# A ring of eight half-expert buffers in a hybrid attention and mixture-of-experts layer

## The chip, the cores and the metric

One core of a Trainium2 chip runs the whole layer in one launch. The metric is device time in microseconds of that core, the median over runs.

## The reference

One layer is applied to 1024 latent tokens and 128 context tokens, width 1024, all in f32. What matters here is its second half:

```python
def hier_moe(h, w_coarse, b_coarse, w_fine, b_fine, w_gate, w_up, w_down):
    ...
    a = (jax.nn.silu(jnp.einsum('td,edf->tef', t, w_gate))
         * jnp.einsum('td,edf->tef', t, w_up) * gates[:, :, None])
    y = jnp.einsum('tef,efd->td', a, w_down)
```

There are 4 groups of 8 experts, 32 in all, with inner width 256. Each token goes to two experts of one group. Ahead of it stand adaLN modulation, windowed attention beside a gated short convolution, and an output projection. Behind it come `x + g2 * moe` and `rmsnorm(x, final_g)`. g2 differs between latent and context tokens.

## The kernel before, in words

**Stages.** Modulation, input projection and attention (to about 382 us), output projection with norm and routing (to 536), the 32 experts (to about 857) and the last stage (to 901). The 1152 tokens are nine tiles of 128; tile 8 holds the context tokens.

**Precision.** A product in f32 is split: `hi` is the value rounded to float32r, `lo` is the rest, and three fast matmuls (hi hi, lo hi, hi lo) take the place of a slow one. So each half of an expert's gate and up weights (128 partitions x 2048 f32, 1 MB) is loaded, ACT writes `gu_hi` (L2165), DVE writes `gu_lo` over the raw half (L2279), and PE runs `products` (L2474 to L2476).

**The ring.** `w_gu` has 3 experts x 2 halves. `gu_hi` has two experts: `gu_hi0` and `gu_hi1`. `w_d` (w_down, 1 MB) has three. The tensors `gu_lo` and `w_gu` share one address, as do `yt` (the nine tiles read back in the last stage) and the raw rings.

**Order by engine.** SP issues nearly all plain DMAs, in program order, and waits there. In the experts' stage its loop is:

```python
for n in range(NE):
    if n + 3 < NE:
        for h in range(2):
            sp.wait_ge(s_gu, 2 * n + h + 1)
            load_gu(n + 3, h)
    if 1 <= n and n + 2 < NE:
        sp.wait_ge(s_down, n)
        load_d(n + 2)
```

`s_gu` counts the halves whose products are done, `s_down` the experts whose `down` is done. PE runs for each expert `gate_up(n, 0)`, `turn_a(n - 1)`, `gate_up(n, 1)`, `turn_x(n + 2)` (eight transposes of gathered rows, L2463), `down(n - 1)` (L2508 to L2518). ACT runs `down_high(n - 1)` (L2195), `turned`, `high(n + 2, 0)`, `silu(n)`, `xhigh(n + 2)`, `high(n + 2, 1)`, `blend(n - 1)` (L2202, which reads the latent row of g2); DVE follows with the low parts, the gated product and `out`. Each engine takes its instructions in order. POOL issues the indirect DMAs: `gather(n + 3)` brings an expert's token rows into `xrows` (a ring of three, L2102), `scatter(n - 2)` writes its results to `y_rows` (L2109). Expert 31 is not scattered: PE adds it from SBUF in the last stage. POOL's descriptors live in a room at the bottom of SBUF, 16384 bytes of a partition.

**Before the experts.** After the last tile's projection PE runs `keep_busy` matmuls (L1860), whose result nobody reads, between waits for DVE's choice of experts: prefix sums (L1904 to L1910), `placed` (L1850, twice: the table of row numbers, then that of gates), and then the first `turn_x`. The first six halves and w_down 0 and 1 are loaded from 505 us on (w_down 2 at 384). SP then waits for the second gather and loads both rows of g2 (1 MB, each row spread over all partitions) and final_g (512 KB).

**Last stage.** When the last scatter has landed, SP loads the nine tiles of `yt` in `ORDER`. POOL or DVE adds the two rows of a token, or PE does; PE adds expert 31, DVE adds the residual (and multiplies by the context g2 for tile 8), ACT and DVE do the final norm with final_g, and SP stores.

Of the kernel before, what the change touches and what calls it, by code (L numbers as in the profile page):

```python
# [41 lines left out]
def build(nc, a):  # L42
# [45 lines left out]
    with root:  # L88
        sb = allocator(root)
        PS = root.enter_context(nc.psum_tensor("PS", [P, 8, 512], F32))  # L90
        ident = sb("ident", [P, P])
# [1132 lines left out]
        s_lo = sem("s_lo")  # L1224
        s_wgu = [[sem(f"s_wgu{i}_{h}") for h in range(2)] for i in range(3)]
# [12 lines left out]
        with ExitStack() as st:  # L1238
# [61 lines left out]
            def mix_sync(sp):  # L1300
                def load_gu(n, h):
                    sp.dma_start(w_gu[:, n % 3, h, :], a["w_gu"][n, h]
                                 ).then_inc(s_wgu[n % 3][h], 16)

                def load_d(n):
                    sp.dma_start(w_d[:, n % 3, :], a["w_down"][n]).then_inc(s_wd[n % 3], 16)

                def load(t):
                    if t >= 2:
                        sp.wait_ge(s_x2, t - 1)  # L1310
                    sp.dma_start(xt[t % 2][:], a["x_all"][:, t, :]).then_inc(s_xt[t % 2], 16)
# [24 lines left out]
                for v, col in ((1, shift_col), (2, gain_col)):  # L1336
                    sp.dma_start(col[:], mod_rows[1, v * D:(v + 1) * D].rearrange(
                        "(k p) -> p k", p=P), allow_slow_non_contiguous=True
                        ).then_inc(s_cols, 16)
                sp.wait_ge(s_pv, NB + 1)  # L1340
                load(0)
                load(1)
                spread_rows(1)
                load_d(2)
                for t in range(LAST):
                    if t + 2 < NT:
                        load(t + 2)
# [444 lines left out]
            def mix_tensor(pe):  # L1792
# [107 lines left out]
                keep_busy(4, 3)  # L1900
# [18 lines left out]
                keep_busy(4, 3)  # L1919
# [49 lines left out]
        ORDER = [4, 5, 0, 1, 8, 6, 2, 3, 7]  # L1969
        DVE_SUM = ORDER[1]  # L1970
        POOL_SUMS = ORDER[2:7]
        with ExitStack() as st:
# [5 lines left out]
            g2row = sb6("g2row", [P, 2, D])  # L1978
            fg = sb6("fg", [P, D])
# [4 lines left out]
            gu_hi = [gu_hi0, sb6("gu_hi1", [P, 2, HALF], F32R)]  # L1984
# [13 lines left out]
            held_hi, held_lo = gu_hi[1][:, 0, 0:D], gu_hi[1][:, 1, 0:D]  # L1998
# [29 lines left out]
            with nc.Block() as block:  # L2028
                @block.sync
                def _(sp):  # L2030
# [3 lines left out]
                    def load_gu(n, h):  # L2034
                        sp.dma_start(w_gu[:, n % 3, h, :], a["w_gu"][n, h]
                                     ).then_inc(s_wgu[n % 3][h], 16)

                    def load_d(n):
                        sp.dma_start(w_d[:, n % 3, :], a["w_down"][n]).then_inc(s_wd[n % 3], 16)

                    sp.wait_ge(s_gx[1], 16)
                    sp.dma_start(g2row[:].rearrange("p c n -> p (c n)"),
                                 mod_g2.to_broadcast([P, 2 * D])).then_inc(s_g2row, 16)
                    sp.dma_start(fg[:], a["final_g"].to_broadcast([P, D])).then_inc(s_p7, 16)
                    for n in range(NE):
                        if n + 3 < NE:
                            for h in range(2):
                                sp.wait_ge(s_gu, 2 * n + h + 1)
                                load_gu(n + 3, h)
                        if 1 <= n and n + 2 < NE:  # L2050
                            sp.wait_ge(s_down, n)
                            load_d(n + 2)

# [103 lines left out]
                def _(act):  # L2157
# [39 lines left out]
                    def blend(n):  # L2197
# [4 lines left out]
                        act.activation(yrows[:, n % 2, :], g2row[:, 0, :], ACT.Identity,  # L2202
# [36 lines left out]
                    def one_round(r):  # L2239
                        def one_expert(e, m):  # L2240
                            act.wait_ge(s_wgu[0][0], 16 * LAP + 16 * m + 16)
                            act.activation(gu_hi[0][:], w_gu[:, 0, :, :], ACT.Copy
# [27 lines left out]
                def _(dve):  # L2270
# [6 lines left out]
                    def low(n, h):  # L2277
                        dve.wait_ge(s_hi, 2 * n + h + 1)
                        dve.tensor_tensor(gu_lo[:, n % 3, h, :], w_gu[:, n % 3, h, :],  # L2279
                                          raw(gu_hi[n % 2][:, h, :]), ALU.subtract  # L2280
# [100 lines left out]
                    def one_round(r):  # L2381
# [9 lines left out]
                        def one_expert(e, m):  # L2391
# [4 lines left out]
                                              raw(gu_hi[0][:]), ALU.subtract  # L2396
# [14 lines left out]
                            dve.tensor_scalar(yrows[:, 0, :], g2row[:, 0, :], onot[:], octx[:],  # L2411
# [11 lines left out]
                    def combine(i, t):  # L2423
# [4 lines left out]
                        if t == NT - 1:  # L2428
                            link(dve.tensor_tensor(x, total, g2row[:, 1, :].rearrange(
# [5 lines left out]
                    def finish(i, t):  # L2435
# [4 lines left out]
                                                 fg[:], ALU.mult, ALU.mult).then_inc(s_fin, 1)  # L2440

                    dve.wait_ge(s_p7, p7_base + 16)
# [10 lines left out]
                def _(pe):  # L2453
# [26 lines left out]
                    def gate_up(n, h):  # L2480
# [7 lines left out]
                        products(PS[:, n % 2, :], gu_hi[n % 2][:, h, :], gu_lo[:, n % 3, h, :],  # L2488
# [62 lines left out]
                    def one_round(r):  # L2551
# [3 lines left out]
                        def one_expert(e, m):  # L2555
# [8 lines left out]
                            for h in range(2):  # L2564
                                last = products(PS[:, 0, :], gu_hi[0][:, h, :], gu_lo[:, 0, h, :],
# [153 lines left out]
```

## Time and profile before

| | us |
|---|---|
| runs of before | 894.86, 905.15, 905.91 |
| median | 905.15 |
| the profiled execution | 903.03 |
| its span, first to last instruction | 900.8 |
| around the span | 2.2 |
| mean granted clock of PE | 0.989 |

The span leaves out 2.2 us at the two ends. In the rows, a time is us from the span's start; L12 is line 12 of the kernel; `x8` is a count of records, where one plain f32 matmul of 512 columns leaves two. `PEclk` 1.00 is the full clock (2.4 GHz) and 0.50 the half (1.2 GHz). `<-` behind "idle" names what ended it. PS is PSUM. SPq is SP's DMA queue.

### The profile page before, as it was taken

The numbers are of one execution on the slowest core, as the hardware profiler recorded it, in microseconds if no ns is written. First come the engines' busy times: TensorE is split into PE (matmuls) and PEld (weight loads), VectorE is DVE, ScalarE is ACT, GpSimd is POOL, SyncE is SP. The second block draws the span as 40 slices with busy tenths as digits, with TensorE's granted clock in tenths as the row PEclk, the third lists the DMA queues.
The fourth block names the chain that finished last, engine by engine and source line by source line (L and its number), as shares of the span: only waits on it lengthen the run. The fifth ranks groups of instructions, "written<-read, shape, count | busy, mean of one in ns | idle before, by whom it ended". The sixth has DMA issues, their size and how long they took to land.

```text
span 900.8 us, 12158 instructions
## 1 busy us (share of the span) xinstructions
PE 863.3 (96%) x4477; PEld 685.4 (76%) x4477; DVE 680.5 (76%) x1018; ACT 461.2 (51%) x693; POOL 229.7 (25%) x210
## 2 busy tenths in 40 slices
PE   4999999999998999999999999999999999999996
PEld 3789999999996555578888667777777767777653
DVE  5557876968856777466888758988888888888678
ACT  6541211111125777534453618786777677776533
POOL 1000000000024777623021231323322332222141
PEclk9899999999999999999999979999999999999999
DMA  9731526424200112152121589999999999998296
GB/s 369 311 120 44 216 67 241 169 89 164 68 29 29 49 48 102 9 210 94 47 94 48 238 290 334 381 381 380 371 379 366 374 371 361 360 366 333 104 377 255
DMA packets 42003, 194.55 MB, mean 216 GB/s; under 512 B 12150, under 2 KB 13110, under 8 KB 25046
## 3 DMA queue, kind: packets, MB, share of 16 engines
q1 hardware_dynamic: 32232, 174.24, 51.5%
q0 software_dynamic: 9712, 19.52, 5.8%
q8 instruction: 37, 0.61, 0.3%
q14 instruction: 22, 0.18, 0.1%
HBM read 182.00 MB, written 26.41 MB: 231 GB/s over the span
## 4 chain that ended last, share of the span: by engine, by line
PE 75%; DMA 7%; DVE 7%; ACT 4%; issue 3%; POOL 2%; POOLq 0%; SPq 0%; DVEq 0%; ACTq 0%
PE PS L968 9%; PE PS L970 8%; PE PS L972 8%; DMA w_gu<-in_w_gu 5%; PE PS L2474 5%; PE PS L2475 5%; PE PS L2476 5%; PE PS L2508 4%; PE PS L1774 3%; PE PS L1776 3%; PE PS L1775 3%; PE PS L1112 3%; PE PS L1081 3%; PE PS L1132 3%; PE PS L2463 2%
## 5 line engine op out<-in xcount | busy, mean ns | idle before, releaser
L2279 DVE TENSOR_TENSOR gu_lo<-w_gu,gu_hi 128x2048 fp32r<-128x2048 f32 x62 | 141.8, 2287 | 28.4 <-ACT gu_hi L2165 28.4
L968 PE MATMUL PS<-h_hi,w_hi 128*128 128x384 f32 (+1 forms) x432 | 148.3, 343 | 2.5 <-DVE h_lo L677 1.9
L2165 ACT ACTIVATE gu_hi<-w_gu 128x2048 fp32r<-128x2048 f32 x62 | 118.9, 1917 | 58.0 <-DMA w_gu<-in_w_gu 57.9
L970 PE MATMUL PS<-h_lo,w_hi 128*128 128x384 f32 (+1 forms) x432 | 147.0, 340 | 0.0
L972 PE MATMUL PS<-h_hi,w_lo 128*128 128x384 f32 (+1 forms) x432 | 146.5, 339 | 0.0
L2474 PE MATMUL PS<-gu_hi,xT_hi 128*128 128x512 f32 x256 | 103.3, 403 | 1.2 <-DVE xT_lo L2338 1.2
L2475 PE MATMUL PS<-gu_lo,xT_hi 128*128 128x512 f32 x256 | 100.4, 392 | 0.0
L2476 PE MATMUL PS<-gu_hi,xT_lo 128*128 128x512 f32 x256 | 100.2, 391 | 0.0
L2109 POOL DMA_INDIRECT y_rows<-yrows,tab x31 | 37.3, 1202 | 211.4 <-DVE yrows L2311 211.4
L968 PEld LDWEIGHTS PS<-h_hi,w_hi 128*128 128x128 f32 x432 | 81.8, 189 | 8.8 <-issue 7.6
L970 PEld LDWEIGHTS PS<-h_lo,w_hi 128*128 128x128 f32 x432 | 82.3, 191 | 0.0
L972 PEld LDWEIGHTS PS<-h_hi,w_lo 128*128 128x128 f32 x432 | 81.9, 190 | 0.0
L484 ACT ACTIVATE w_hi<-w_raw 128x1024 fp32r<-128x1024 f32 x16 | 16.9, 1056 | 96.2 <-PE PS L972 64.7
L2508 PE MATMUL PS<-w_d,aT 128*128 128x512 f32 x128 | 60.3, 594 | 0.4 <-ACT aT L2185 0.4
L1774 PE MATMUL PS<-wo_hi,cat_hi 128*128 128x512 f32 x144 | 58.6, 407 | 1.3 <-ACT att L1447 1.3
L2102 POOL DMA_INDIRECT xrows<-h_rows,tabg x29 | 53.2, 1834 | 16.4 <-PE PS L2463 8.5
L1776 PE MATMUL PS<-wo_hi,cat_lo 128*128 128x512 f32 x144 | 56.9, 395 | 0.0
L1775 PE MATMUL PS<-wo_lo,cat_hi 128*128 128x512 f32 x144 | 56.9, 395 | 0.0
L2474 PEld LDWEIGHTS PS<-gu_hi,xT_hi 128*128 128x128 f32 x256 | 48.4, 189 | 10.8 <-issue 1.3
L2476 PEld LDWEIGHTS PS<-gu_hi,xT_lo 128*128 128x128 f32 x256 | 48.0, 188 | 11.0
L2475 PEld LDWEIGHTS PS<-gu_lo,xT_hi 128*128 128x128 f32 x256 | 48.2, 188 | 9.1
L451 POOL TENSOR_SCALAR probs<-probs,inv 128x512 f32<-128x512 f32 (+2 forms) x72 | 45.7, 650 | 36.5 <-DVE inv L893 36.4
(290 smaller groups left out, 1746.7 us busy)
## 6 DMA issues: line engine op xcount, KB each, us to landing
w_gu<-in_w_gu SPq DMA_DIRECT2D x64, 1024.0 KB, 13.8
w_d<-in_w_down SPq DMA_DIRECT2D x32, 1024.0 KB, 13.3
wm<-in_w_mod SPq DMA_DIRECT2D x16, 1024.0 KB, 5.3
w_raw<-in_w_in SPq DMA_DIRECT2D x18, 512.0 KB, 6.3
yt<-y_rows SPq DMA_DIRECT2D x9, 1024.0 KB, 15.2
xt<-in_x_all SPq DMA_DIRECT2D x9, 512.0 KB, 3.6
y_all<-yt SPq DMA_DIRECT2D x9, 512.0 KB, 3.0
wm<-in_w_mod SPq DMA_DIRECT2D x2, 2048.0 KB, 12.5
```

The costliest lines, as they stand in the source:

```text
L968: pe.matmul(o, w_hi[b][:, k, :], h_hi[:, k, tok], start=k == 0, stop=False)
L970: pe.matmul(o, w_hi[b][:, k, :], h_lo[:, k, tok], start=False, stop=False)
L972: last = pe.matmul(o, w_lo[b][:, k, :], h_hi[:, k, tok], start=False, stop=k == KD - 1)
L1774: pe.matmul(o, cat_hi[b][:, k, :], wh, start=k % 4 == 0, stop=False)
L1775: pe.matmul(o, cat_hi[b][:, k, :], wl, start=False, stop=False)
L1776: last = pe.matmul(o, cat_lo[b][:, k, :], wh, start=False, stop=k % 4 == 3)
L2165: act.activation(gu_hi[n % 2][:, h, :], w_gu[:, n % 3, h, :], ACT.Copy).then_inc(s_hi, 1)
L2279: dve.tensor_tensor(gu_lo[:, n % 3, h, :], w_gu[:, n % 3, h, :], raw(gu_hi[n % 2][:, h, :]), ALU.subtract).then_inc(s_lo, 1)
L2474: pe.matmul(o, xT_hi[:, x, kk, :], hi[:, cols], start=kk == 0, stop=False)
L2475: pe.matmul(o, xT_hi[:, x, kk, :], lo[:, cols], start=False, stop=False)
L2476: last = pe.matmul(o, xT_lo[:, x, kk, :], hi[:, cols], start=False, stop=kk == KD - 1)
L2508: pe.matmul(PS[:, 5 + half, :], aT[:, n % 2, 1, :], w_d[:, n % 3, cols], start=True, stop=False)
```

## The change

The ring of halves gets eight slots. Slots 0 to 5 stay in `w_gu`. Slot 6 takes the place of `final_g`'s tile and of the second row of g2; slot 7 takes 8 KB of a partition from POOL's descriptor room, which goes from 16384 to 8192 bytes. Half i is in slot i % 8 and its load waits for the products of half i - 8. `gu_hi` still has four halves and `w_d` three experts. Half 7 is loaded in the output projection stage, half 6 after the first gather. SP loads only the latent row of g2 before the experts; final_g and the context row of g2 go into two slots of `xrows` when all 32 `turn_x` are done. `keep_busy` ahead of the prefix sums has six matmuls for four, and the last one three for four. `ORDER` of the last stage becomes 0, 1, 2, 3, 8, 4, 5, 6, 7. The loop over experts for overflow (not taken with these inputs) is changed in names only.

```diff
+        with ExitStack() as same:
+            gu_raw7 = allocator(same)("gu_raw7", [P, 2 * D])
+        gu_lo7 = sb("gu_lo7", [P, 2 * D], F32R)
...
                 load_d(2)
+                sp.dma_start(gu_raw7[:], a["w_gu"][3, 1]).then_inc(s_half7, 16)
                 for t in range(LAST):
...
                 pe.wait_ge(s_comb, NT + 1)
-                keep_busy(4, 3)
+                keep_busy(6, 3)
                 pe.wait_ge(s_both, 4)
...
                 placed(PS[:, 2, 0:NE], 3, slice(1, 2), first=False).then_inc(s_gatesum, 1)
-                keep_busy(4, 3)
+                keep_busy(3, 3)
...
-        ORDER = [4, 5, 0, 1, 8, 6, 2, 3, 7]
+        ORDER = [0, 1, 2, 3, 8, 4, 5, 6, 7]
+        RING, HIGHS = 8, 4
+        GU_LAP = len(range(0, 2 * NE, RING))
+        s_half = [*(s for pair in s_wgu for s in pair), s_xt[0], s_half7]
+        half_base = [0] * 6 + [16 * (NT - NT // 2), 0]
...
-            g2row = sb6("g2row", [P, 2, D])
-            fg = sb6("fg", [P, D])
+            g2row = sb6("g2row", [P, D])
+            with ExitStack() as same:
+                gu_raw6 = allocator(same, "right")("gu_raw6", [P, HALF])
+            gu_lo6 = sb6("gu_lo6", [P, HALF], F32R)
+            fg, g2_ctx = xrows[:, 1, :], xrows[:, 2, :]
...
+            def raw_half(i):
+                s = i % RING
+                return w_gu[:, s // 2, s % 2, :] if s < 6 else [gu_raw6, gu_raw7][s - 6][:]
...
+            def high_half(i):
+                return (gu_hi1 if i % HIGHS >= 2 else gu_hi0)[:, i % 2, :]
...
+                    def load_half(i):
+                        sp.dma_start(raw_half(i), a["w_gu"][i // 2, i % 2]
+                                     ).then_inc(s_half[i % RING], 16)
...
+                    sp.wait_ge(s_gx[0], 16)
+                    for i in range(6, 7):
+                        load_half(i)
                     sp.wait_ge(s_gx[1], 16)
-                    sp.dma_start(g2row[:].rearrange("p c n -> p (c n)"),
-                                 mod_g2.to_broadcast([P, 2 * D])).then_inc(s_g2row, 16)
-                    sp.dma_start(fg[:], a["final_g"].to_broadcast([P, D])).then_inc(s_p7, 16)
+                    sp.dma_start(g2row[:], mod_g2[:, 0:D].to_broadcast([P, D])
+                                 ).then_inc(s_g2row, 16)
                     for n in range(NE):
-                        if n + 3 < NE:
-                            for h in range(2):
-                                sp.wait_ge(s_gu, 2 * n + h + 1)
-                                load_gu(n + 3, h)
+                        for i in (2 * n, 2 * n + 1):
+                            if i + RING < 2 * NE:
+                                sp.wait_ge(s_gu, i + 1)
+                                load_half(i + RING)
                         if 1 <= n and n + 2 < NE:
                             sp.wait_ge(s_down, n)
                             load_d(n + 2)
+                    sp.wait_ge(s_turnx, NE)
+                    sp.dma_start(fg, a["final_g"].to_broadcast([P, D])).then_inc(s_p7, 16)
+                    sp.dma_start(g2_ctx, mod_g2[:, D:2 * D].to_broadcast([P, D])
+                                 ).then_inc(s_p7, 16)
...
-                            sp.wait_ge(s_gu, 2 * (NE - [2, 1, 3][t // 2] + 1))
+                            sp.wait_ge(s_gu, max(i for i in range(2 * NE) if i % RING == t) + 1)
...
                     def high(n, h):
-                        act.wait_ge(s_wgu[n % 3][h], 16 * (n // 3 + 1))
-                        if n >= 2:
-                            act.wait_ge(s_gu, 2 * (n - 2) + h + 1)
-                        act.activation(gu_hi[n % 2][:, h, :], w_gu[:, n % 3, h, :], ACT.Copy
-                                       ).then_inc(s_hi, 1)
+                        i = 2 * n + h
+                        loaded_half(act, i)
+                        if i >= HIGHS:
+                            act.wait_ge(s_gu, i - HIGHS + 1)
+                        act.activation(high_half(i), raw_half(i), ACT.Copy).then_inc(s_hi, 1)
...
-    nc = bacc.Bacc("TRN2", target_bir_lowering=False, num_devices=1)
+    nc = bacc.Bacc("TRN2", target_bir_lowering=False, num_devices=1,
+                   dynamic_dma_scratch_size=8192)
```

## Rows read from the trace of the kernel before

**Rows 1.** The page: span, PE, GB/s in 40 slices, chain by engine
```profile
span 900.8 us, 12158 instructions
...
PE 863.3 (96%) x4477; PEld 685.4 (76%) x4477; DVE 680.5 (76%) x1018; ACT 461.2 (51%) x693; POOL 229.7 (25%) x210
...
GB/s 369 311 120 44 216 67 241 169 89 164 68 29 29 49 48 102 9 210 94 47 94 48 238 290 334 381 381 380 371 379 366 374 371 361 360 366 333 104 377 255
...
PE 75%; DMA 7%; DVE 7%; ACT 4%; issue 3%; POOL 2%; POOLq 0%; SPq 0%; DVEq 0%; ACTq 0%
```

**Rows 2.** Windows of the experts' stage: us, busy PE, PEld, DVE, ACT, POOL, clock, DMA, GB/s
```profile
563.00:600.00 37.00, 37.00 (x169) 28.51 (x168) 32.95 (x29) 28.34 (x32) 11.73 (x8) 1.00 1.00 383
760.00:800.00 40.00, 39.38 (x174) 28.98 (x174) 33.42 (x28) 28.85 (x31) 12.45 (x8) 1.00 0.97 365
```

**Rows 3.** Waits from 536 to 901: in total, times, longest
```profile
ACT gu_hi L2165 <- DMA w_gu<-in_w_gu: 57.9, 22, 3.4
```

**Rows 4.** Chain that ended last, `turn_x` of experts 3, 13 and 29
```profile
573.08 0.89 PE PS L2463 x8
...
670.55 0.89 PE PS L2463 x8
...
832.21 0.89 PE PS L2463 x8
```

**Rows 5.** Timeline of SP's queue, three issues of the experts' stage
```profile
579.85 3.33 SPq L2035 DMA_DIRECT2D w_gu<-in_w_gu  x2
586.85 0.33 SPq L2039 DMA_DIRECT2D w_d<-in_w_down  x1
589.60 3.33 SPq L2035 DMA_DIRECT2D w_gu<-in_w_gu  x2
```

**Rows 6.** Timeline of ACT, one expert
```profile
599.91 1.92 ACT L2165 ACTIVATE gu_hi<-w_gu 128x2048 fp32r<-128x2048 f32 x1
...
607.11 1.05 ACT L2195 ACTIVATE wd_hi<-w_d 128x1024 fp32r<-128x1024 f32 x1
```

**Rows 7.** DMA issues from 783 to 803: count, KB, median us to landing
```profile
w_gu<-in_w_gu SPq DMA_DIRECT2D x4, 1024.0 KB, 15.3
w_d<-in_w_down SPq DMA_DIRECT2D x2, 1024.0 KB, 14.3
...
y_rows<-yrows,tab POOLq DMA_INDIRECT x2, 8.7
```

**Rows 8.** DMA issues from 563 to 583
```profile
y_rows<-yrows,tab POOLq DMA_INDIRECT x2, 9.3
```

**Rows 9.** Timeline of PE in the routing stage
```profile
513.39 3.60 PE L1860 MATMUL PS<-cat,ident 128*128 128x512 f32 x8
...
518.50 0.46 PE L1904 MATMUL PS<-both,before 128*128 128x96 f32 x2 [1.51 <-DVE both L1613]
```

**Rows 10.** Chain that ended last, routing stage: start, us, what
```profile
521.79 4.11 PE PS L1850 x20
525.90 4.64 PE PS L1860 x6
530.54 2.15 PE PS L1850 x20
532.70 3.52 PE PS L1860 x8
```

**Rows 11.** Window 520 to 525, columns as in rows 2
```profile
520.00:525.00 5.00, 5.00 (x20) 3.97 (x19) 1.67 (x3) 0.00 (x0) 0.00 (x0) 0.50 1.02 428
```

**Rows 12.** Timeline of POOL, first gathers and the clearing scatter
```profile
527.83 1.09 POOL L1394 DMA_INDIRECT xrows<-h_rows,tabg  x1 [11.85 <-DVE tabg L1744]
529.23 2.02 POOL L1394 DMA_INDIRECT xrows<-h_rows,tabg  x1 [0.30 <-issue]
...
534.83 1.27 POOL L2093 DMA_INDIRECT y_rows<-yrows,tab  x1 [0.82 <-POOL yrows L2091]
```

**Rows 13.** Timeline of SP's queue, behind the wait for the second gather
```profile
535.45 0.33 SPq L2042 DMA_DIRECT2D g2row<-mod_g  x1
```

More of the change, by code:

```diff
@@ L1224, in build @@
         s_lo = sem("s_lo")
+        s_half7 = sem("s_half7")
         s_wgu = [[sem(f"s_wgu{i}_{h}") for h in range(2)] for i in range(3)]
@@ L1983, in build @@
             sb6("gu_hi0_again", [P, 2, HALF], F32R)
-            gu_hi = [gu_hi0, sb6("gu_hi1", [P, 2, HALF], F32R)]
+            gu_hi1 = sb6("gu_hi1", [P, 2, HALF], F32R)
             xT_hi = sb6("xT_hi", [P, 2, KD, P], F32R)
@@ L1997, in build, with low_half, loaded_half @@
             held_id = sb6("held_id", [P, 1])
-            held_hi, held_lo = gu_hi[1][:, 0, 0:D], gu_hi[1][:, 1, 0:D]
+            held_hi, held_lo = gu_hi1[:, 0, 0:D], gu_hi1[:, 1, 0:D]
+            def raw_half(i):
+                s = i % RING
+                return w_gu[:, s // 2, s % 2, :] if s < 6 else [gu_raw6, gu_raw7][s - 6][:]
+            def low_half(i):
+                s = i % RING
+                return gu_lo[:, s // 2, s % 2, :] if s < 6 else [gu_lo6, gu_lo7][s - 6][:]
+            def high_half(i):
+                return (gu_hi1 if i % HIGHS >= 2 else gu_hi0)[:, i % 2, :]
+            def loaded_half(eng, i):
+                eng.wait_ge(s_half[i % RING], half_base[i % RING] + 16 * (i // RING + 1))
             def held_rows(t):
@@ L2201, in blend @@
                             act.wait_ge(s_zero, 16)
-                        act.activation(yrows[:, n % 2, :], g2row[:, 0, :], ACT.Identity,
+                        act.activation(yrows[:, n % 2, :], g2row[:], ACT.Identity,
                                        bias=of_ctx[:, n:n + 1], scale=no_ctx[:, n:n + 1]
@@ L2240, in one_expert @@
                         def one_expert(e, m):
-                            act.wait_ge(s_wgu[0][0], 16 * LAP + 16 * m + 16)
-                            act.activation(gu_hi[0][:], w_gu[:, 0, :, :], ACT.Copy
+                            act.wait_ge(s_wgu[0][0], 16 * GU_LAP + 16 * m + 16)
+                            act.activation(gu_hi0[:], w_gu[:, 0, :, :], ACT.Copy
                                            ).then_inc(s_hi, 1)
@@ L2278, in low @@
                         dve.wait_ge(s_hi, 2 * n + h + 1)
-                        dve.tensor_tensor(gu_lo[:, n % 3, h, :], w_gu[:, n % 3, h, :],
-                                          raw(gu_hi[n % 2][:, h, :]), ALU.subtract
+                        i = 2 * n + h
+                        dve.tensor_tensor(low_half(i), raw_half(i), raw(high_half(i)), ALU.subtract
                                           ).then_inc(s_lo, 1)
@@ L2395, in one_expert @@
                             dve.tensor_tensor(gu_lo[:, 0, :, :], w_gu[:, 0, :, :],
-                                              raw(gu_hi[0][:]), ALU.subtract
+                                              raw(gu_hi0[:]), ALU.subtract
                                               ).then_inc(s_lo, 1)
@@ L2410, in one_expert @@
                             dve.sem_inc(s_pass, 1)
-                            dve.tensor_scalar(yrows[:, 0, :], g2row[:, 0, :], onot[:], octx[:],
+                            dve.tensor_scalar(yrows[:, 0, :], g2row[:], onot[:], octx[:],
                                               ALU.mult, ALU.add).then_inc(s_blend, 1)
@@ L2428, in combine @@
                         if t == NT - 1:
-                            link(dve.tensor_tensor(x, total, g2row[:, 1, :].rearrange(
+                            link(dve.tensor_tensor(x, total, g2_ctx.rearrange(
                                 "p (k n) -> p k n", k=KD), ALU.mult))
@@ L2439, in finish @@
                         dve.scalar_tensor_tensor(yt[:, t, 0, :], yt[:, t, 0, :], fss[:, t, 2:3],
-                                                 fg[:], ALU.mult, ALU.mult).then_inc(s_fin, 1)
-                    dve.wait_ge(s_p7, p7_base + 16)
+                                                 fg, ALU.mult, ALU.mult).then_inc(s_fin, 1)
+                    dve.wait_ge(s_p7, p7_base + 32)
                     dve.wait_ge(s_yt[DVE_SUM], yt_base + 16)
@@ L2487, in gate_up @@
                                 pe.wait_ge(s_a, n - 1)
-                        products(PS[:, n % 2, :], gu_hi[n % 2][:, h, :], gu_lo[:, n % 3, h, :],
+                        products(PS[:, n % 2, :], high_half(2 * n + h), low_half(2 * n + h),
                                  n % 2, h).then_inc(s_gu, 1)
@@ L2564, in one_expert @@
                             for h in range(2):
-                                last = products(PS[:, 0, :], gu_hi[0][:, h, :], gu_lo[:, 0, h, :],
+                                last = products(PS[:, 0, :], gu_hi0[:, h, :], gu_lo[:, 0, h, :],
                                                 0, h)
```

3 lines of the change are left out of this document (removed).

## The prediction

> **What bounds the kernel now.** I read the page first [rows 1]. The span is 900.8 us and the chain that ended last is 75% PE, 7% DMA, 7% DVE: mostly a PE-bound kernel, with waits between. The GB/s line has 40 slices of 22.5 us, counted here from 0; from slice 25 (563 us) to slice 35 it reads 360 to 381, nearly flat. So the experts' stage runs against two limits at once. The stage windows show the same [rows 2]: at 563 to 600 the DMA engines are busy all the time at 383 GB/s, and at 760 to 800 they give 365 GB/s while PE has small holes.
>
> The waits come next [rows 3]: ACT waited 22 times, 57.9 us together, for a half of the gate and up weights. Most of that is hidden. What is not hidden is read from the chain, by the eight transposes of `turn_x` that close an expert's second half [rows 4]: expert 3 at 573.08, expert 13 at 670.55, expert 29 at 832.21. The first ten periods are (670.55 - 573.08) / 10 = 9.747 us, PE's own pace. Sixteen more would end at 670.55 + 155.95 = 826.50; they ended at 832.21. **5.7 us** are lost there to late weights, all behind expert 13.
>
> Why late: a transfer into a half of the ring may only start when that half's products are done. For a first half that ACT uses at 599.91 [rows 6], the load went out at 589.60 [rows 5], 10.3 us before. PE starts to slip when a load needs some 14 us, so about 4 us past the normal time of use are absorbed. In the late experts a load takes 15.3 us [rows 7].
>
> The second place is the routing stage before the experts. PE is idle for 1.51 us before the prefix matmuls at 518.50 [rows 9], and then the granted clock is 0.50 in the window 520 to 525 [rows 11], the lower level (1.2 GHz). The chain stays on PE there up to the first `turn_x` at 536.2 [rows 10].
>
> **The change part by part.** *Two more halves in the ring.* The load of half i+8 now goes out when the products of half i are done, where i+6 did before. In steady state that is one expert (two halves) earlier: 579.85 in place of 589.60 for the same use at 599.91 [rows 5, 6], so 20.1 us of lead in place of 10.3, and 24 with the 4 that are absorbed. The number of loads issued up to a moment stays the same, so the DMA queue is as full as before at each moment; only what it carries is needed later. Is 24 enough? Latency at 783 to 803 is 15.3 us [rows 7], held down by PE's slip. Without the slip the queue gets longer by at most all of it: 15.3 + 5.7 = 21.0. That is below 24, so the whole 5.7 us can go. The next thing late would be w_down: its ring of three is not deepened. Its load at 586.85 [rows 5] is used at 607.11 [rows 6], a lead of 20.3 us, with some 3 us more absorbed because PE needs it only in the next `down`; its latency would be 14.3 + 5.7 = 20.0 [rows 7]. It just fits. I allow 0.5 us for the last experts and take **-5.2**, ends 0 and -5.7.
>
> *Where the two halves come from.* Half 7 is loaded in the output projection stage, 1.05 MB or 2.7 us at the 383 GB/s of rows 2, in slice 17, where the page's line shows 210 GB/s [rows 1]; ahead of the next token tile in the queue, which has far longer until its use. Half 6 (1 MB) goes out after the first gather and the one g2 row (512 KB) after the second, against g2's 1 MB and final_g's 512 KB before: 1.5 MB both. final_g and the second g2 row (1 MB, 2.7 us) move behind the last w_down load, into the slice of 104 GB/s (slice 37, [rows 1]); they are used at the end, over 30 us later. All this costs 0; uncovered, each would be 2.7 us.
>
> *Half of POOL's descriptor room.* No row shows the limit. From one side: POOL issued three gathers and a scatter from 527.83 to 534.83 with about 0.3 us between gathers [rows 12], and the second gather had landed only by 535.45, when SP got past its wait [rows 13]. So the full room held at least two that had not landed, probably four; in steady state a scatter and a gather are out together. I take 0, near what these rows show. The other end is the last rival. 
>
> *Matmuls that keep PE busy.* Before the prefix matmuls six stand where four stood, at the end three in place of four. Four (8 pieces) take 3.52 us at full clock [rows 10], 0.88 each. Two more run to about 513.39 + 3.60 + 1.76 = 518.75 [rows 9], so the prefix is 0.25 late but the hole of 1.51 us is gone. If the clock then stays at the higher level (2.4 GHz): the first table's 20 matmuls take 2.15 and not 4.11 us, the three busy matmuls after it (6 pieces) 2.64 and not 4.64, and the one ahead of it, by the same price, 0.88 and not 1.55 [rows 10]. That is 1.96 + 0.67 - 0.25 = 2.4 before the table is read; then 2.0, and 0.88 for the matmul dropped: 5.3 on PE. But the first `turn_x` also needs the first gather. It was issued at 527.83 [rows 12], now at 525.4; the second took at most 535.45 - 529.23 = 6.2 us to land [rows 12, 13], so the first arrives by 531.6 and `turn_x` starts some 4.4 us before its 536.2. I take **-4.3**, ends +0.3 (clock still drops, and the dropped matmul hides nothing) and -5.3. The Trainium skill (TensorE: Matmul & The Clock Gate, What's actually happening) says that the lower clock is the default which activity lifts, and that where the change falls moves from run to run. The trace agrees that the drop follows a hole; by the second half of the rule the drop may still come in some executions, as in rival (a).
>
> *The new order of the last stage* keeps the context tile fifth and nine loads of 1 MB in a row, all behind the last scatter: 0. Where six of the tiles come free earlier, none waited on that.
>
> **Sum.** 903.03 - 5.2 - 4.3 = **893.5 us**. The profiled execution lies 2.1 below the median of 905.15; one run of before is at 894.86, which could be an execution without the clock drop and with little slip, and then it would gain little.
>
> **The rivals.** (a) *Only the ring pays, the clock still drops* (another hole, or the small-column matmuls of the table let it fall): 903.03 - 5.2 - 0.6 (0.88 less 0.25) = 897.2. For it: window 520 to 525 holds mostly short matmuls. Against: the same 20 matmuls at 530.54 ran at full clock. (b) *The wait moves to w_down or the DMA rate itself*: the lead grows but the queue in front of w_down is as long; if all 5.7 stay: 903.03 - 4.3 = 898.7. For: 20.0 against 20.3. Against: its slack of about 3. (c) *Neither works*, 903. (d) *More than forecast*: the run at 894.86 is the true floor of before and both savings come on top, 894.86 - 9.5 = 885.4. (e) *Slower: the halved room holds one indirect DMA at a time.* Then each gather waits for the scatter before it, 8.7 us [rows 7], and lands about as long after: 17.4 us an expert in place of 9.75, 28 times 7.7 = 214 us, so about 1117. It decides once fewer than two fit; with two it costs under 2 us at the start. Against: the four of rows 12.
>
> **How the numbers follow.** Forecast 0.46, (a) 0.22, (b) 0.13, (c) 0.07, (d) 0.09, (e) 0.03. Two per cent of the median, 18.1 us, is about what a measurement of this kernel can tell: faster than 887.0 is only (d), 0.09; slower than 923.3 only (e), 0.03; the rest 0.88. The range goes from 887.5 (part of d) to 901.5, which takes in (a) and (b), and leaves out (c), (e) and most of (d).
>
> **What would show it.** Right: `turn_x` periods of 9.75 us to expert 29 (255.9 us from expert 3 to 29 or hardly more, 259.1 now); weight latency rising to 19 to 21 us late in the stage, yet ACT's waits of 57.9 us nearly gone; no clock of 0.50 between 510 and 535; the first `turn_x` near 532; 1 MB more traffic in slice 17 and in slice 37. Wrong: ACT or PE waiting for w_down; a clock of 0.5 again at 520; gaps of over 0.3 us between POOL's issues that end with a landing; a longer wait for the first gather.

## The result, and the profile after

| | before | after |
|---|---|---|
| median, first set of runs | 900.94 (15 runs, 894.86 to 906.09) | **893.12** (15 runs, 891.95 to 900.43) |
| ratio to before, 95% interval | | 0.9934 [0.9908, 0.996] |
| median, second set | 901.2 (19 runs) | 893.88 (12 runs, 892.14 to 899.89) |
| ratio to before, 95% interval | | 0.9929 [0.9902, 0.9955] |
| the profiled execution | 903.03 | 892.42 |
| its span | 900.8 | 890.2 |

The change saves some 6 to 8 us of 901, a clear gain but far inside the 2 per cent. The forecast was 893.5.

The page of the profile after (span, busy time of the engines, GB/s in 40 slices, chain by engine, and the group of ACT's conversions of the halves in `w_gu`, whose last two fields are the idle time ahead of it and what ended it):

```profile
span 890.2 us, 12163 instructions
...
PE 855.3 (96%) x4479; PEld 684.5 (77%) x4479; DVE 678.7 (76%) x1018; ACT 466.0 (52%) x693; POOL 232.9 (26%) x210
...
GB/s 368 321 124 46 215 61 250 156 104 166 68 29 16 52 36 127 9 260 71 72 71 72 145 345 353 378 388 378 374 374 370 374 381 368 372 374 288 147 387 250
...
PE 83%; DVE 6%; ACT 3%; issue 2%; POOL 2%; DMA 2%; POOLq 0%; SPq 0%; DVEq 0%; ACTq 0%
...
L2198 ACT ACTIVATE gu_hi<-w_gu 128x2048 fp32r<-128x2048 f32 x46 | 88.1, 1915 | 0.0
```

Against [rows 1] the chain has 83% PE where it had 75%, and DMA's share fell from 7% to 2%. ACT's 57.9 us of waiting for weights [rows 3] are 0.0. Slice 17 carries 260 GB/s for 210 (half 7), slice 37 carries 147 for 104 (final_g and the context row): 1.1 and 0.9 MB more. Slice 22 has 145 for 238 only because slices are shorter: it ends at 512 us where it ended at 518, and the weights' loads begin near 505.

The experts' stage in windows, columns as in [rows 2]:

```profile
563.00:600.00 37.00, 37.00 (x169) 28.46 (x168) 33.00 (x28) 28.14 (x32) 12.45 (x8) 1.00 0.99 387
760.00:800.00 40.00, 40.00 (x183) 30.96 (x182) 34.92 (x30) 30.74 (x35) 12.63 (x9) 1.00 0.99 371
```

PE is busy for all 40.00 us of the second, where [rows 2] had 39.38. The chain that ended last, `turn_x` of experts 3, 13 and 29, against [rows 4]:

```profile
568.05 0.89 PE PS L2495 x8
...
665.58 0.89 PE PS L2495 x8
...
821.66 0.89 PE PS L2495 x8
```

The first ten periods are 9.753 us (9.747 before), and the sixteen behind them now 9.755 each, with no slip. From expert 3 to 29 it is 253.61 us for 259.13: **5.5 us**. The issues from 780 to 800 us show the latency, the time from a load's issue to its landing, that PE no longer feels (count, KB, median us to landing; compare [rows 7]):

```profile
w_gu<-in_w_gu SPq DMA_DIRECT2D x3, 1024.0 KB, 20.0
...
y_rows<-yrows,tab POOLq DMA_INDIRECT x3, 8.8
```

A half takes 20.0 us from issue to landing for 15.3, and nothing waits for it. A scatter still takes 8.8 us.

The routing stage on PE after, against [rows 9, 10] (start, us, what, idle before):

```profile
510.45 3.50 PE L1901 MATMUL PS<-xt,h2T 128*128 128x128 f32 x16
513.79 5.32 PE L1865 MATMUL PS<-cat,ident 128*128 128x512 f32 x12
518.94 0.41 PE L1909 MATMUL PS<-both,before 128*128 128x96 f32 x2
...
520.97 0.97 PE L1855 MATMUL PS<-entry,near 128*128 128x32 f32 x8
522.15 1.52 PE L1855 MATMUL PS<-entry,near 128*128 128x32 f32 x12 [0.20 <-DVE near L1667]
523.51 2.82 PE L1865 MATMUL PS<-cat,ident 128*128 128x512 f32 x6
526.17 2.31 PE L1855 MATMUL PS<-entry,near 128*128 128x32 f32 x20
528.32 2.82 PE L1865 MATMUL PS<-cat,ident 128*128 128x512 f32 x6
530.98 1.05 PE L2495 MATMUL PS<-ident,xrows 128*128 128x128 f32 x8
```

The hole of 1.51 us ahead of the prefix matmuls is gone and the first table runs at full clock. But the half clock did not leave this profile: it came earlier.

Windows of the profile after, columns as in [rows 2]; the second stands against [rows 11]:

```profile
510.00:515.00 5.00, 5.00 (x24) 4.36 (x24) 2.47 (x10) 3.61 (x3) 0.00 (x0) 0.66 1.01 426
...
520.00:525.00 5.00, 4.80 (x28) 3.49 (x28) 2.72 (x10) 0.00 (x0) 0.00 (x0) 1.00 1.02 420
```

The clock of 0.66 lies over the matmuls of L1901, which took 3.50 us. In the profile before the same matmuls, and the first `turn_x`, stand so:

```profile
511.55 2.00 PE L1896 MATMUL PS<-xt,h2T 128*128 128x128 f32 x16
...
536.05 1.05 PE L2463 MATMUL PS<-ident,xrows 128*128 128x128 f32 x8
```

The first `turn_x` starts at 530.98 for 536.05 before. Some 1.2 us of these 5.1 had been gained ahead of routing, where no part of the change works: from 20 to 40 us the granted clock is 0.83 in the profile before and 0.91 in this one, which had less of the half clock there. Routing itself gave 3.8. Between the first `turn_x` and expert 3 both profiles need the same (37.07 and 37.03), and behind expert 29 too (68.54 and 68.59). So the two spans differ by 10.6 = 1.2 + 3.8 + 5.5, to 0.1.

POOL and SP in the profile after, against [rows 12, 13]:

```profile
525.62 1.09 POOL L1399 DMA_INDIRECT xrows<-h_rows,tabg  x1 [9.24 <-DMA h_rows<-h]
527.01 2.00 POOL L1399 DMA_INDIRECT xrows<-h_rows,tabg  x1 [0.31 <-issue]
529.32 3.10 POOL L1399 DMA_INDIRECT xrows<-h_rows,tabg  x1 [0.30 <-issue]
```

```profile
530.37 0.33 SPq L2061 DMA_DIRECT2D gu_raw<-in_w_gu  x1
```

The gaps between POOL's gathers are 0.3 us as before, with half the room. Half 6 goes out at 530.37, once the first gather has landed.

### The profile page after: what moved, and what is told of

Read it like the earlier page. It is cut to its first block, busy times and chain, and to the rows that moved or that the text cites. A ratio compares the mean times of both kernels' runs of the same rounds, so it can differ in the third digit from the quotient of the medians.

```text
span 890.2 us, 12163 instructions
## 1 busy us (share of the span) xinstructions
PE 855.3 (96%) x4479; PEld 684.5 (77%) x4479; DVE 678.7 (76%) x1018; ACT 466.0 (52%) x693; POOL 232.9 (26%) x210
## 4 chain that ended last, share of the span: by engine, by line
PE 83%; DVE 6%; ACT 3%; issue 2%; POOL 2%; DMA 2%; POOLq 0%; SPq 0%; DVEq 0%; ACTq 0%
PE PS L971 9%; PE PS L973 8%; PE PS L975 8%; PE PS L2506 6%; PE PS L2507 6%; PE PS L2508 6%; PE PS L2540 6%; PE PS L1779 3%; PE PS L1781 3%; PE PS L1780 3%; PE PS L2495 3%; PE PS L1115 3%; PE PS L1084 3%; PE PS L1135 3%; PE PS L2547 2%
## 5 line engine op out<-in xcount | busy, mean ns | idle before, releaser
L2312 DVE TENSOR_TENSOR gu_lo<-w_gu,gu_hi 128x2048 fp32r<-128x2048 f32 x46 | 105.1, 2284 | 2.3 <-ACT gu_hi L2198 1.5
L2198 ACT ACTIVATE gu_hi<-w_gu 128x2048 fp32r<-128x2048 f32 x46 | 88.1, 1915 | 0.0
L2343 DVE TENSOR_TENSOR yrows<-PS,yrows 128x1024 f32<-128x1024 f32 x32 | 39.2, 1224 | 40.9 <-ACT yrows L2234 34.5
```

The source lines that it names most:

```text
L2198: act.activation(high_half(i), raw_half(i), ACT.Copy).then_inc(s_hi, 1)
L2312: dve.tensor_tensor(low_half(i), raw_half(i), raw(high_half(i)), ALU.subtract).then_inc(s_lo, 1)
```

## The experiments

The granted clock over the whole span differs between executions of one program. They are split here at 0.992. Over all executions whose clock is on record (the first set of before has none):

| | executions | at or above 0.992: median, mean | below: number, median | mean of all |
|---|---|---|---|---|
| before | 77 | 898.67, 898.38 | 39, 902.67 | 900.85 |
| after | 27 | 893.01, 893.23 | 7, 898.61 | 894.61 |

The 39 are 4 us longer in the median, and 14 of them, below 0.9865, 7 us (905.6). The profile of before that the prediction rests on has clock 0.989: it is one of the 39.

The split serves as a measure of the clock drop in what follows, with two limits. First, the mean over the span says how much clock was missing and not where. The profiles show the half clock at several places, two of them far ahead of everything that the change touches. This is the clock of the page (slices of 22.5 us, counted from 0) for before, experiment 8 and experiment 9 (both described below):

```profile
PEclk9899999999999999999999979999999999999999
PEclk9899999999999999999999998999999999999999
PEclk9899999999999999999999999999999999999999
```

Slice 1 is low in all three; only slice 23 of before and slice 24 of experiment 8 are routing and the first experts. From 20 to 40 us the clock was 1.00 in the profile of experiment 1, 0.91 in that of after and 0.83 in that of before, and the router's matmuls, which end the last tile, started at 502.45, 503.63 and 504.86: 1.2 us a step. Five profiles (experiments 3, 5, 6, 7 and 8) have 0.91 from 280 to 300 us too, worth some 1.9 us (506.72 in experiment 8 for 504.86 in before, both with 0.83 in the first place). So part of what parts the two groups has nothing to do with routing. Second, the 77 come from three chips, whose executions at or above 0.992 have medians of 898.26, 899.44 and 896.56: chips differ by up to 3 us.

**1. The fillers alone.** Theory: the fillers give 4.3 us. Rival: the clock falls anyway, and they give nearly nothing.

```diff
 # before.py
-                keep_busy(4, 3)
+                keep_busy(6, 3)
...
-                keep_busy(4, 3)
+                keep_busy(3, 3)
```

> The kernel before with the matmul fillers of the change alone (six and three for four and four). Theory A (two additive parts: fewer clock drops in routing, and no slip behind expert 13): the slip of about 5.5 us from expert 3 to 29 stays (259 us, not 253.6), the executions with a low clock around 520 become fewer, the median falls to about 897. Rival B (the fillers do nothing, the ring gives it all): median as the kernel before, about 901. Rival C (the fillers give it all): about 893.

Measured: median 898.6 (12 runs), ratio 0.9975 [0.9946, 1.0004]. Only 3 of 12 executions are below 0.992. The mean is 899.40, 1.45 below that of before, with a 95% interval of 2.1 to either side. The slip is untouched, 258.20 us from expert 3 to 29 (chain that ended last):

```profile
566.03 0.89 PE PS L2463 x8
...
824.23 0.89 PE PS L2463 x8
```

So the fillers may be worth some 1.5 us on average, but this run doesn't part that from nothing: the interval takes in 1. It does rule out the 4.3 of the forecast as an average.

**2. The ring alone.**

```diff
 # after.py
-                keep_busy(6, 3)
+                keep_busy(4, 3)
...
-                keep_busy(3, 3)
+                keep_busy(4, 3)
```

> The changed kernel with the four and four fillers of before. Theory A: expert 3 to 29 takes 253.6 us, the routing stage drops its clock as often as before, times in two groups near 893 and 899, median 896 to 899. Rival B (ring gives all): 893. Rival C (fillers give all): 901.

Measured: median 895.71 (12 runs), ratio 0.9944 [0.9912, 0.9975]; mean 896.29, 4.56 below before. Six of 12 are below 0.992, as in before; the other six have a median of 893.13, close to the 893.01 of after. The chain:

```profile
573.27 0.89 PE PS L2495 x8
...
826.88 0.89 PE PS L2495 x8
```

253.61 us, exactly that of after. The ring removes the slip by itself. In this profile the half clock is back at its old place (0.50 from 520 to 525 us). The two parts add up: 4.56 + 1.45 = 6.0, against 6.24 for both.

**3. A ring of seven.** The half from the descriptor room is given up, the one in place of final_g and g2's second row stays.

```diff
 # after.py
-            gu_raw7 = allocator(same)("gu_raw7", [P, 2 * D])
-        gu_lo7 = sb("gu_lo7", [P, 2 * D], F32R)
...
-        ORDER = [0, 1, 2, 3, 8, 4, 5, 6, 7]
-        RING, HIGHS = 8, 4
+        ORDER = [1, 2, 3, 4, 8, 5, 6, 0, 7]
+        RING, HIGHS = 7, 4
...
-    nc = bacc.Bacc("TRN2", target_bir_lowering=False, num_devices=1,
-                   dynamic_dma_scratch_size=8192)
+    nc = bacc.Bacc("TRN2", target_bir_lowering=False, num_devices=1)
```

> The changed kernel with seven halves: slot 7 and its early load are left out, POOL's descriptor room is back at 16384 bytes. The lead of a load over its use is 15.2 us plus some 4 absorbed, against latencies that reach 20 us with eight halves. Theory A: a small slip remains at the end, 0 to 1.5 us from expert 3 to 29, time 893 to 895. Rival D (the first MB loaded early counts as much as the depth): slip of about 3 us, 896.

Measured: median 894.11 (6 runs, none below 0.992), ratio 0.9918 [0.9888, 0.9948]. Chain, then waits (in total, times, longest):

```profile
568.55 0.89 PE PS L2491 x8
...
823.65 0.89 PE PS L2491 x8
```

```profile
ACT gu_hi L2194 <- DMA w_gu<-in_w_gu: 27.9, 16, 2.8
...
ACT gu_hi L2194 <- DMA gu_raw<-in_w_gu: 4.8, 2, 3.1
```

255.10 us: a slip of 1.7 (the expectation had up to 1.5), with ACT waiting 32.7 us. The latency late in the stage stops at 18.3 us, where eight halves let it rise to 20.0. Seven slots give some 4.0 of the 5.5 us; the eighth, with its early load, is worth the rest (this run gives up both and doesn't part them). The slip of seven comes late: PE is busy for 40.00 us from 720 to 760 and for 39.53 from 760 to 800. Against the 893.01 of after's undisturbed clock the median is 1.1 us longer, which fits a slip of 1.7.

**4. A room of 1024 bytes.** Does the descriptor room cost anything, alone? A sixteenth of it; the pad holds the addresses of everything else where they were.

```diff
 # before.py
+        sb("room_pad", [P, 3840])
...
-    nc = bacc.Bacc("TRN2", target_bir_lowering=False, num_devices=1)
+    nc = bacc.Bacc("TRN2", target_bir_lowering=False, num_devices=1,
+                   dynamic_dma_scratch_size=1024)
```

> The kernel before with 1024 bytes of descriptor room per partition instead of 16384, and nothing else changed (the rest of the space is left empty). Theory A (the room costs nothing at 8192 because few descriptors are out at a time): even an eighth of that costs at most 2 us at the first three gathers, 901 to 903. Rival E (the room holds few indirect DMAs, and the halving is near the limit): gathers wait for landings, over 950 us.

Measured: median 900.71 (10 runs), ratio 1.0004 [0.9971, 1.0038]. POOL's timeline:

```profile
525.78 2.90 POOL L1395 DMA_INDIRECT xrows<-h_rows,tabg  x1 [9.84 <-issue]
528.99 3.02 POOL L1395 DMA_INDIRECT xrows<-h_rows,tabg  x1 [0.30 <-issue]
532.31 0.99 POOL L1395 DMA_INDIRECT xrows<-h_rows,tabg  x1 [0.30 <-issue]
...
535.29 1.03 POOL L2094 DMA_INDIRECT y_rows<-yrows,tab  x1 [1.02 <-issue]
```

Three gathers and a scatter go out one behind the other, no gap ends with a landing, and in the whole experts' stage POOL waits for no landing. Rival (e) has no ground even at an eighth of the room that the change leaves.
This profile also prices the drop in routing. It has the old fillers and the old hole of 1.51 us, and the clock stayed at 1.00 there. From the start of the `w_gain` matmuls (509.71) to the first `turn_x` (532.04) it took 22.3 us, where the profile before took 26.3 (509.75 to 536.05). So the drop cost 4.0 us in that execution; where it doesn't come, the new fillers have hardly anything to give: 22.5 us in the profile after, 22.2 in that of experiment 9.

**5. The late rows alone.** final_g and the context row of g2 go out behind the loop over experts, in the old ring.

```diff
 # before.py
-                    sp.dma_start(g2row[:].rearrange("p c n -> p (c n)"),
-                                 mod_g2.to_broadcast([P, 2 * D])).then_inc(s_g2row, 16)
-                    sp.dma_start(fg[:], a["final_g"].to_broadcast([P, D])).then_inc(s_p7, 16)
+                    sp.dma_start(g2row[:, 0, :], mod_g2[:, 0:D].to_broadcast([P, D])
+                                 ).then_inc(s_g2row, 16)
...
+                    sp.dma_start(fg[:], a["final_g"].to_broadcast([P, D])).then_inc(s_p7, 16)
+                    sp.dma_start(g2row[:, 1, :], mod_g2[:, D:2 * D].to_broadcast([P, D])
+                                 ).then_inc(s_p7, 16)
...
-                    dve.wait_ge(s_p7, p7_base + 16)
+                    dve.wait_ge(s_p7, p7_base + 32)
```

> The kernel before, ring of six, with final_g and the context row of g2 loaded behind the last w_down load instead of ahead of the experts. Theory A (depth of the ring is what removes the slip; the DMA engines ran idle near 555 us, so 1 MB less ahead of that is lost): the slip from expert 3 to 29 stays at about 5.5 us (259 us), time as the kernel before, near 901. Rival D (the transfers moved out of the stage give much of the gain): slip down by up to 2.7 us, 898.5.

Measured: median 902.37 (12 runs), ratio 1.0001 [0.9973, 1.0028]. Expert 3 to 29 took 257.5 us in this profile, a slip of 4.1, where the other ring-of-six profiles have 4.8 to 6.0. Perhaps 1 MB less ahead of the experts takes some slip away; the time doesn't show it, and seven of the 12 were below 0.992, which clouds a gain of one us. So most of the 5.5 us does not come from the lateness of the rows.

**6. How much lead there is.** Three copies of 1 MB that nobody needs go into SP's queue at expert 8 of the changed kernel. Each makes the queue longer for all that is behind it.

```diff
 # after.py
+    spare = nc.dram_tensor("spare", (3, P, 2 * D), F32, kind="Internal").ap()
...
+                        if n == 8:
+                            for m in range(3):
+                                sp.dma_start(spare[m], a["w_gu"][m, 0]).then_inc(s_p5, 16)
...
+                    sp.wait_ge(s_p5, 112)
                     sp.wait_ge(s_turnx, NE)
```

> The changed kernel with three extra copies of 1 MB each from DRAM to DRAM in SP's queue at expert 8, 8.2 us of DMA work at 383 GB/s. Theory A (a load may take some 23 to 24 us before PE slips, and eight halves end at 20): latencies would go to 28 late in the stage, so PE slips by about 4.5 us, 253.6 becomes about 258, time near 897.5; the wait that shows up first is ACT's for w_down or w_gu. Rival F (the ring has slack to spare): no slip, 893. Rival G (no slack, DMA is the bound): the full 8.2 us, 901.

Measured: median 896.5 (11 runs), ratio 0.9952 [0.9933, 0.9972]. Chain; then issues from 780 to 800; then waits:

```profile
575.47 0.89 PE PS L2500 x8
...
833.55 0.89 PE PS L2500 x8
```

```profile
w_gu<-in_w_gu SPq DMA_DIRECT2D x4, 1024.0 KB, 24.8
w_d<-in_w_down SPq DMA_DIRECT2D x2, 1024.0 KB, 24.0
```

```profile
ACT gu_hi L2203 <- DMA w_gu<-in_w_gu: 34.4, 19, 2.4
...
ACT wd_hi L2232 <- DMA w_d<-in_w_down: 5.2, 13, 0.7
```

258.08 us, a slip of 4.7 for 4.5 expected. The ring of eight stops the rise of latency at 24.8 us, where the prediction put its lead at 24; w_down's loads reach 24.0 us with no wait over 0.7, so its lead with slack (20.3 + 3 in the prediction) is a little larger than thought. So the change has a reserve of 4.8 us of latency left (24.8 less 20.0), and by this run gate and up weights would be late first. The median moved by 3.4 us against after (at or above 0.992 the mean moved by 2.8), where the one profile slipped by 4.7 (4.5 more than after); whether the other executions slipped less stays open.

**7. No fillers ahead of the prefix sums.**

```diff
 # after.py
                 pe.wait_ge(s_comb, NT + 1)
-                keep_busy(6, 3)
                 pe.wait_ge(s_both, 4)
```

> The changed kernel without the six fillers ahead of the prefix matmuls (a hole of about 5 us on PE). Theory A (a hole there lets the clock fall): nearly all executions at a granted clock of 0.985 to 0.990, 897 to 901. Rival B (the clock falls for other reasons): as the changed kernel, most at 892.8.

Measured: median 895.62 (12 runs), ratio 0.9934 [0.991, 0.9958]. Eight of 12 are below 0.992, and only five at 0.989 or less: the expectation of nearly all was half missed. The profiled execution (900.84, PE idle for 5.04 us ahead of the prefix sums):

```profile
520.00:525.00 5.00, 3.08 (x11) 2.64 (x12) 2.42 (x11) 0.21 (x1) 0.00 (x0) 0.50 1.01 398
525.00:530.00 5.00, 5.00 (x22) 4.44 (x21) 1.15 (x2) 0.00 (x0) 0.00 (x0) 0.50 0.95 400
```

The half clock lasts these 10 us and some more here, and the execution is among the longest. But four executions of this kernel, not profiled, took 891.95 to 893.35, like the best of after. So without the fillers the drop is likelier (8 of 12 for 7 of 27), but the hole doesn't decide it.

**8. After again.** The changed kernel once more, to see how often it drops and where.

> The changed kernel as it is, again. Theory A: two groups, three in four near 892.8 and one in four at 897 to 900; median 893. Against the kernel before the ratio should come out at 0.991 to 0.994.

Measured: median 893.88 (12 runs), ratio 0.9929 [0.9902, 0.9955]; three of 12 below 0.992. The profiled one took 899.89, clock 0.987:

```profile
510.00:515.00 5.00, 4.04 (x27) 3.84 (x28) 2.49 (x12) 2.79 (x6) 0.00 (x0) 0.82 1.02 426
515.00:520.00 5.00, 5.00 (x19) 3.33 (x19) 3.19 (x10) 3.32 (x2) 0.61 (x1) 0.84 1.00 421
...
535.00:545.00 10.00, 8.22 (x31) 6.73 (x32) 3.58 (x3) 3.26 (x4) 6.05 (x5) 0.66 0.86 290
```

The drop comes ahead of the fillers, before 520, and once more at the first experts, 535 to 545. From expert 3 on this execution is like the other: 253.62 us to expert 29. Of the 7.5 us by which it is longer, 3.1 were lost ahead of the last tile's end (506.72 for 503.63, with the drops of slice 1 and of 280 to 300 us), 1.5 in routing, and 2.9 between the first `turn_x` and expert 3.

**9 and 10. A filler further up.** In the profile after, PE idles for 0.87 us ahead of the `w_gain` matmuls (L1821) and then comes the clock of 0.66. (The same hole stands in the profile before, where the clock stayed at 1.00 from 510 to 515 us.) Does a filler there help? The kernel ran twice.

```diff
 # after.py
                 turn_last(1)
+                keep_busy(1, 0)
                 pe.wait_ge(s_gstd, NT)
```

> The changed kernel with one more filler in the hole of 0.87 us behind the second half's transposes of the last tile (near 507.7). Theory A (the drops that are left come from that hole): the share of executions near 899 (4 of 15) goes to none or nearly, median 892.6. Rival (they come from elsewhere): the share stays a quarter.

> The kernel with one more filler near 507.7 again, beside the changed kernel on one chip. Theory A: executions near 899 are none or fewer than one in ten, median 892.6. Rival (0 of 6 was chance): a quarter of them near 899, as the changed kernel had.

Measured: 892.55 (6 runs, 892.01 to 893.42), ratio 0.9904 [0.9881, 0.9927]; again 892.43 (6 runs, 891.57 to 893.29), ratio 0.991 [0.9875, 0.9945]. None of the 12 is below 0.992. Timeline of PE, then two windows, of the first:

```profile
508.65 1.02 PE L1865 MATMUL PS<-cat,ident 128*128 128x512 f32 x2
509.69 1.97 PE L1821 MATMUL PS<-w_gain,h2T 128*128 128x64 f32 x16
...
531.89 1.13 PE L2496 MATMUL PS<-ident,xrows 128*128 128x128 f32 x8 [1.20 <-DMA xrows<-h_rows,tabg]
```

```profile
510.00:515.00 5.00, 5.00 (x35) 4.10 (x35) 3.23 (x12) 3.10 (x4) 0.00 (x0) 1.00 1.01 424
...
520.00:525.00 5.00, 4.80 (x27) 3.40 (x26) 3.00 (x12) 0.00 (x0) 0.00 (x0) 1.00 1.01 423
```

The hole of 0.87 is filled and the clock is 1.00 through the stage. Yet the first `turn_x` is no earlier than in the profile after, counted from the `w_gain` matmuls (22.2 us for 22.5), since it now waits 1.20 us for the first gather, as the prediction said that it would. So the drop at 510 to 514 cost that profile almost nothing. This is the version that I would keep; its mean is 892.5 against 894.6 for after, though the ratios to before overlap in their intervals.

**11. And one filler behind the first `turn_x`**, where PE waits 1.2 us for `xT_lo` and near which the execution of experiment 8 had its second drop.

```diff
 # experiment 9 and
                     turn_x(0)
+                    pe.matmul(PS[:, 7, :], ident[:], cat[:, 0:4, 0:P], start=True, stop=True)
```

> The changed kernel with two more fillers: one in the hole of 0.87 us near 507.7, one in the hole of 1.2 us between the first transposes and the first products of the experts. Theory A (each hole there gives the clock a chance to fall in some executions): no or nearly no execution below a granted clock of 0.994, median 892.6 or a little less. Rival (only the first hole matters): the same as the kernel with one more filler. Rival H (the filler delays the products): 893.5.

Measured: median 893.25 (8 runs), ratio 0.9918 [0.9887, 0.995], none below 0.992. No better than without it: no gain of the second of the two fillers can be seen.

## Why the prediction was right or wrong

The forecast of 893.5 is 0.4 from the median of 893.12. It hit through one right term and two errors that cancel.

**The ring, -5.2: right.** Between expert 3 and 29 the profiles differ by 5.5 us. Among executions at or above 0.992 the means differ by 898.38 - 893.23 = 5.15; within one chip it is 4.7 (experiment 2) and 3.7 (experiment 8). The mechanism stands too: latency late in the stage 20.0 (the bound was 21.0), the lead 24.8 by experiment 6 (24 was worked out), w_down at 17.9 us in the issues of 760 to 780 and never waited for. Ring alone gives the whole of it (experiment 2), seven slots part of it (3), late rows alone none that a measurement shows (5). One figure of "What would show it" was an arithmetic slip: 26 periods of 9.747 us are 253.4, not 255.9. Measured 253.6. "The number of loads issued up to a moment stays the same" holds only for the loads issued within the stage; halves 6 and 7 come on top, but have landed by 538 us, so the queue is as full as before (8.5 to 8.9 us to landing at 563 to 583, 8.6 before).

**Where the halves come from, 0, and the room, 0: right.** No wait of POOL for a landing among its first issues, none of ACT in the experts' stage for a half of either store, final_g and the rows at 826 us with over 30 us to go. Experiment 4 bounds the room far below what the change uses.

**The deeper queue beside the gathers, 0: right**, 8.8 us for a scatter against 8.7.

**The fillers, -4.3: the step that failed by its size.** The working of the stage was good: prefix at 518.94 (518.75 predicted), three busy matmuls 2.82 (2.64), first `turn_x` at 530.98 (531.6 to 532). In the pair of profiles routing gave 3.8 us, in spite of a clock of 0.66 at 510 to 515, because the first gather would have held `turn_x` back anyway (experiment 9). That the prefix came at 518.94 is in part luck: all was 1.2 us early, and then that drop took 1.5. The sign "no clock of 0.50 between 510 and 535" did not hold: from 511 to 513 us it is 0.50. But the 4.3 were priced from one execution, in which the clock fell in routing, as though it fell there in all. It doesn't: the profile of experiment 4 has the old fillers and no drop there, and only 39 of 77 executions have a mean clock below 0.992, drops at other places included. The excess that the drops add to the mean was 900.85 - 898.38 = 2.47 us before and 894.61 - 893.23 = 1.38 after: 1.1 saved. Experiment 1 gives 1.45, after against experiment 2 gives 1.7, both with some 2.1 us to either side. So the term was 1.1 to 1.7 us by the best estimate, perhaps nothing, and near 4 only for an execution that drops in routing. The rival (a), the clock still drops, is true of at most 7 of 27 executions; their median of 898.61 is near its 897.2, but part of it is lost elsewhere, as experiment 8 shows.

**The base, 903.03: too high.** It is an execution with the drop; 900.96 is the median of the 77. By that base the same sum would be 891.5. The error of the base (2.1) and that of the fillers (some 2.8) nearly cancel. The text had a hint, the run at 894.86, and read it as "without the clock drop and with little slip"; the drop was right, but it left the base where it was.

The Trainium skill (TensorE: Matmul & The Clock Gate, What's actually happening) had it that activity lifts the clock and that the place of the change moves from run to run. The runs bear out the second half: among the profiles of the changed kernel the half clock lay near 510 to 514 in one, and near 513 to 517 and again from 535 to 545 in the other. Of the first half they show that the clock came back while PE was busy (5.00 of 5.00 us from 530 to 535 in experiment 7, where it rose from 0.50 to 1.00); what starts a drop they don't show.

**The rivals.** (b) is out: in the profile after nobody waits for w_down. (c) is out by the interval. (d), both on top of a floor of 894.86, is out: the lowest of after is 891.95. (e) is out by experiment 4. **The last stage's order, 0**: 68.54 us from expert 29 to the end for 68.59.

## What to carry to other kernels

A slip that builds up slowly (a steady period, then a longer one) is a ring whose lead is below the latency of a full queue: compare the lead of each load, its release to its use plus what is absorbed, with the latency it would have without the slip, and the gain follows, here to a few tenths in the profiles (5.2 forecast, 5.5 measured). Where a profiled execution shows a granted clock below full in some stretch, first ask how many executions do, from the clock of each run, and weigh the price by that share; take as base the median of many, not that one execution. The clock of a whole run lumps all places together, so look in more than one profile for the place. A store kept for one late use (final_g, the second row) and a room that is larger than its users need are good places to take a ring slot from.

## What the runs showed of the hardware

- The same program has a mean clock below 0.992 in about half of its executions (39 of 77 of before), which are 4 us longer in the median, and 7 us the 14 with the lowest clock. The half clock comes at several places: 20 to 40 us, 280 to 300, routing, the first experts. The drop in routing alone cost 4.0 us in the profile before.
- Short holes go with the drops but don't decide them. Behind the hole of 1.51 us the clock fell in the profile before and stayed at 1.00 in that of experiment 4; behind the hole of 0.87 us it fell in the profile after and stayed at 1.00 in that of before. With both filled 0 of 20 executions fell below 0.992 (experiments 9 to 11), with the second alone filled 7 of 27, with a hole of 5.04 us 8 of 12. That the filler at 508.65 is the cause is likely and not shown: were the two kernels alike, all seven would fall on the 27 with a chance of 1 to 2 in 100, and the clock of a whole run doesn't part routing from the places ahead of it.
- A descriptor room of 1024 bytes of a partition carries 64 indirect DMAs of 128 rows without a wait, ratio 1.0004 [0.9971, 1.0038].
- The latency of a load late in the stage is bounded by how far ahead the ring lets it be issued: at 780 to 800 us it is 15.2 us with six halves, 18.3 with seven, and 24.8 with eight and 3 MB more. With eight alone it is 20.0 and no bound: nothing waits, and it was 18.5 from 760 to 780. The rate between 780 and 800 us is 367 to 374 GB/s whatever the ring. Why seven stop at 18.3, below the middle of 20.0 between six and eight, wasn't tried; their slip had only just begun.
